# A fused encoder block on one core: turning the next tile's input before the query projection, router steps right behind their turns, and a reordered set of first loads

## The reference

```python
hn   = rmsnorm(h, norm_mix)
b_gate, c_gate, x_in, c_q, c_kv, k_pe = split(hn @ w_in)        # 512,512,512,384,256,64
conv = b_gate * dwconv3_causal(c_gate * x_in)
q    = rmsnorm(c_q) @ w_uq  ;  k_nope, v = rmsnorm(c_kv) @ w_ukv # 4 heads; q, k normed per head, rope
attn = softmax(q k^T / sqrt(192), chunk-causal) v
h    = h + concat([conv, attn]) @ w_o
h    = h + MoE(rmsnorm(h))      # router on 32 experts, the best 4, clamped SwiGLU, gates from a softmax
```

## Time and profile before

| | us |
|---|---|
| median of 3 runs (lowest to highest) | 2258.73 (2258.47 to 2261.2) |
| profiled execution, its own time | 2259.32 |
| its span | 2257.5 |
| PE busy / PEld busy | 2088.5 / 1886.0 |
| DVE / ACT / POOL busy | 738.0 / 443.9 / 556.3 |
| mean granted clock | 0.971 |

### The profile page before, as it was taken

How to read it: one execution, slowest core, us unless ns; L and a number is a source line. 1 busy time by engine, 2 the same in 40 slices (tenths; PEclk the granted TensorE clock), 3 DMA queues, 4 the chain that set the end, 5 groups by cost and what they waited for, 6 DMA issues and landing times.

```text
span 2257.5 us, 41903 instructions
## 1 busy us (share of the span) xinstructions
PE 2088.5 (93%) x15574; PEld 1886.0 (84%) x15575; DVE 738.0 (33%) x1949; ACT 443.9 (20%) x1078; POOL 556.3 (25%) x637
## 2 busy tenths in 40 slices
PE   6888889999994999999999999999999999999991
PEld 5666666675553899999999999999999999999991
DVE  1222222233343333433333333333333433343331
ACT  1222233232321111111111111111111111111110
POOL 1111101110024223232322323223232322323321
PEclk9999999999996999999999999999999999999996
DMA  7000000033421889999999999999999989999997
GB/s 264 10 10 10 10 10 10 1 124 91 130 67 37 279 275 311 325 302 290 291 294 277 305 301 277 317 287 305 287 307 315 320 275 277 316 319 318 306 292 86
DMA packets 308020, 486.97 MB, mean 216 GB/s; under 512 B 107984, under 2 KB 129360, under 8 KB 307920
## 3 DMA queue, kind: packets, MB, share of 16 engines
q1 hardware_dynamic: 250608, 437.49, 59.4%
q0 software_dynamic: 33120, 44.91, 9.6%
q10 hardware_dynamic: 24240, 3.85, 1.1%
HBM read 454.83 MB, written 35.84 MB: 217 GB/s over the span
## 4 chain that ended last, share of the span: by engine, by line
PE 90%; DVE 3%; issue 2%; ACT 2%; DMA 1%; POOL 1%; ACTq 0%; DVEq 0%; SPq 0%; POOLq 0%
PE psum L989 42%; PE psum L1005 22%; PE psum L790 8%; PE psum L938 5%; PE psum L825 2%; PE psum L881 2%; PE psum L828 2%; PE psum L918 2%; PE psum L897 2%; PE psum L805 1%; PE psum L870 1%; PE psum L896 1%; DMA area<-in_w_in 1%; PE psum L968 1%; DVE area L1115 0%
## 5 line engine op out<-in xcount | busy, mean ns | idle before, releaser
L989 PE MATMUL psum<-area 128*128 128x128 f32 (+3 forms) x8192 | 978.8, 282 | 36.5 <-issue 18.8
L989 PEld LDWEIGHTS psum<-area 128*128 128x128 f32 x8192 | 970.3, 192 | 41.8 <-issue 41.5
L1005 PE MATMUL psum<-area 128*128 128x128 f32 (+3 forms) x4096 | 496.3, 282 | 0.9
L1005 PEld LDWEIGHTS psum<-area 128*128 128x128 f32 x4096 | 484.5, 191 | 10.0 <-DVE area L1285 8.7
L1266 DVE TENSOR_SCALAR area<-psum,area 128x160 f32<-128x160 f32 x256 | 86.4, 379 | 612.6 <-PE psum L989 612.6
L588 POOL DMA_INDIRECT sum_rows<-area x165 | 261.1, 1582 | 67.3 <-issue 40.2
L749 ACT ACTIVATE area<-area 128x320 f32<-128x320 f32 x128 | 60.1, 470 | 734.2 <-DVE area L1266 734.2
L790 PE MATMUL psum<-area 128*128 128x128 f32 x1536 | 175.9, 275 | 3.5 <-ACT area L662 1.2
L790 PEld LDWEIGHTS psum<-area 128*128 128x128 f32 x1536 | 173.4, 192 | 5.0 <-ACT area L666 1.7
L578 POOL DMA_INDIRECT area<-normed_rows,area x165 | 160.5, 973 | 61.4 <-issue 61.4
L573 POOL TENSOR_TENSOR area<-area 128x5 uint32<-128x5 uint32 x33 | 6.3, 190 | 620.8 <-DVE area L1251 575.0
(11 more groups left out here) (180 smaller groups left out, 1314.0 us busy)
## 6 DMA issues: line engine op xcount, KB each, us to landing
area<-in_w_gate_up SPq DMA_DIRECT2D x256, 1024.0 KB, 6.5
area<-in_w_down SPq DMA_DIRECT2D x128, 1024.0 KB, 7.1
area<-in_w_in SPq DMA_DIRECT2D x3, 2048.0 KB, 13.0
area<-in_x SPq DMA_DIRECT2D x9, 512.0 KB, 11.1
area<-in_w_o SPq DMA_DIRECT2D x1, 4096.0 KB, 13.1
sum_rows<-area SPq DMA_DIRECT2D x32, 128.0 KB, 3.0
normed_rows<-area SPq DMA_DIRECT2D x8, 512.0 KB, 3.3
out<-sum_rows SPq DMA_DIRECT2D x4, 1024.0 KB, 13.9
```

The costliest lines, as they stand in the source:

```text
L989: ins = mm(dst, w_gu[piece][:, k, c * P:(c + 1) * P], xT[:, PART * s + k, 0:width], start=(s == 0 and k == 0 and c % 2 == 0), stop=(s == 1 ...
L1005: ins = mm(bank[4 + d // 3][:, (d % 3) * SLOTS:(d % 3) * SLOTS + width], w_dn[q][:, kk, d * P:(d + 1) * P], actT[:, 2 * q + kk, 0:width], ...
```

## The change

Four things change. (1) In the loop over the tiles, HNa and HNb of the next tile stand before UQ, HNa between TPa and S, HNb behind PV, and UKV follows UQ directly. The last PV of a tile stands behind X. (2) At the end, the router step RT of a tile stands right behind its turns HB, ahead of the second half of WO. (3) SyncE's first loads: the constants come in two pieces (the first holds the identity and eps), the low block of `w_in` in two halves of four k-rows, each with a semaphore, and the large blocks follow at once. g_mix is issued by ScalarE, the seven small loads by GpSimd, which then waits for `w_ukv` before it writes the zeros and lists. LOW takes the k-rows by halves for both banks. (4) ScalarE does a small Sqrt before anything else. The zeros are taken from `attnT` instead of `v_sb`, so that the wait for their writes moves from UKV(0) on ScalarE to PV(3) on VectorE.

The diff, cut to its core; left out are the declarations of the new semaphores, the other small loads (moved in the same manner), and waits on `rest_in` before the first ranks and before VectorE's use of the token numbers:

```diff
@@ constants
         "ident": np.eye(P, dtype=np.float32),
+        "eps": np.full((P, 1), EPS, np.float32),
...
@@ schedule(), the loop over the eight token tiles
         if i > 1:
-            steps += unit(old + 3)[1:]
+            steps += unit(old + 3)[1:-1]
         steps.append(("X", i))
+        if i > 1:
+            steps.append(("PV", old + 3))
...
         steps.append(("BC", i))
         if i:
-            steps += unit(new)
+            steps.append(("TPa", new))
         if i + 1 < NT:
             steps.append(("HNa", i + 1))
         if i:
-            steps.append(("SC", new + 1))
-        steps.append(("UQ", i))
+            steps += unit(new)[1:]
         if i + 1 < NT:
             steps.append(("HNb", i + 1))
-        steps.append(("UKV", i))
+        if i:
+            steps.append(("SC", new + 1))
+        steps += [("UQ", i), ("UKV", i)]
...
-    steps += [("WO", 4), ("RT", 0), ("HA", 1), ("HB", 1), ("WO", 5), ("RT", 1), ("HA", 2)]
+    steps += [("WO", 4), ("RT", 0), ("HA", 1), ("HB", 1), ("RT", 1), ("WO", 5), ("HA", 2)]
     for i in range(3, e):
-        steps += [("WO", 2 * i), ("HB", i - 1), ("WO", 2 * i + 1), ("RT", i - 1), ("HA", i)]
+        steps += [("WO", 2 * i), ("HB", i - 1), ("RT", i - 1), ("WO", 2 * i + 1), ("HA", i)]
@@ SyncE
             sp.dma_start(xt, x_rows[0]).then_inc(x_in, 16)
-            sp.dma_start(consts[:], consts_dram).then_inc(consts_in, 16)
-            sp.dma_start(g_mix[:], I["norm_mix"][0].rearrange("(k p) -> p k", p=P), allow_slow_non_contiguous=True).then_inc(g_mix_in, 16)
-            sp.dma_start(w_in[:, :, 3 * CONV:], w_in_v[:, :, 3 * CONV:]).then_inc(w_low_in, 16)
-            sp.dma_start(g_q[:, 0:NCQ], I["q_norm"][0].rearrange("(k p) -> p k", p=P), allow_slow_non_contiguous=True).then_inc(small_in, 16)
...
+            sp.dma_start(consts[:, 0:P + 1], consts_dram[:, 0:P + 1]).then_inc(consts_in, 16)
+            for k in (0, KD // 2):
+                sp.dma_start(w_in[:, k:k + KD // 2, 3 * CONV:], w_in_v[:, k:k + KD // 2, 3 * CONV:]).then_inc(w_low_in[2 * k // KD], 16)
+            sp.dma_start(consts[:, P + 1:], consts_dram[:, P + 1:]).then_inc(rest_in, 16)
             sp.dma_start(w_in[:, :, CONV:2 * CONV], w_in_v[:, :, CONV:2 * CONV]).then_inc(w_c_in, 16)
@@ GpSimd
+            g.memset(stat[:, 39:40], 0.0).then_inc(warm_ready, 1)
...
-            zeros = v_sb[:, 0:2, :].rearrange("p a n -> p (a n)")
+            zeros = attnT[:, HEADS - 1, :]
             g.memset(zeros, 0.0).then_inc(zero_ready, 1)
             wait(zero_ready, 2)
+            pool.dma_start(g_q[:, 0:NCQ], I["q_norm"][0].rearrange("(k p) -> p k", p=P), allow_slow_non_contiguous=True).then_inc(small_in, 16)
...
+            wait(w_ukv_in, 16)
             for dram in (hf_dram, acc_dram):
...
-            wait(consts_in, 16)
+            wait(rest_in, 16)
             wait(small_in, 16 * 7)
@@ ScalarE
+            act.dma_start(g_mix[:], I["norm_mix"][0].rearrange("(k p) -> p k", p=P), allow_slow_non_contiguous=True).then_inc(g_mix_in, 16)
+            act.wait_ge(warm_ready, 1)
+            A(stat[:, 38:39], stat[:, 39:40], ACT.Sqrt)
             act.wait_ge(consts_in, 16)
...
-                    if n == 0:
-                        act.wait_ge(zero_out, 16 * 4)
@@ VectorE, step PV
+                    if n == HEADS - 1:
+                        dve.wait_ge(zero_out, 16 * 4)
@@ TensorE, step LOW
-                    for k in range(KD):
-                        mm(bank[2][:, 0:QL], hnT[:, k, :], w_in[:, k, 3 * CONV:3 * CONV + QL],
-                           start=(k == 0), stop=(k == KD - 1))
...
+                    for half in range(2):
+                        if n == 0:
+                            pe.wait_ge(w_low_in[half], 16)
+                        for bk, a, b in ((bank[2], 0, QL), (bank[3], QL, LOW)):
+                            for k in range(4 * half, 4 * half + 4):
+                                ins = mm(bk[:, 0:b - a], hnT[:, k, :], w_in[:, k, 3 * CONV + a:3 * CONV + b],
+                                         start=(k == 0), stop=(k == KD - 1))
```

More of the change, by code:

```diff
@@ L346, in build @@
         w_dn_v = I["w_down"][0].rearrange("e (k p) n -> e p k n", p=P)
-        consts_in, g_mix_in, small_in, x_in = sem("consts_in"), sem("g_mix_in"), sem("small_in"), sem("x_in")
-        w_low_in, w_c_in, w_x_in, w_b_in, w_uq_in, w_ukv_in = (sem(n) for n in ("w_low_in", "w_c_in", "w_x_in", "w_b_in", "w_uq_in", "w_ukv_in"))
+        consts_in, rest_in, warm_ready = sem("consts_in"), sem("rest_in"), sem("warm_ready")
+        g_mix_in, small_in, x_in = sem("g_mix_in"), sem("small_in"), sem("x_in")
+        w_low_in = [sem(f"w_low_in{half}") for half in range(2)]
+        w_c_in, w_x_in, w_b_in, w_uq_in, w_ukv_in = (sem(n) for n in ("w_c_in", "w_x_in", "w_b_in", "w_uq_in", "w_ukv_in"))
         x_sq, in_std, in_rstd, hn_ready = sem("x_sq"), sem("in_std"), sem("in_rstd"), sem("hn_ready")
@@ L519, in rotate @@
                 return g.tensor_tensor(dst, tmp[:, 0:heads * ROPE], tmp[:, heads * ROPE:2 * heads * ROPE], ALU.add)
-            zeros = v_sb[:, 0:2, :].rearrange("p a n -> p (a n)")
+            zeros = attnT[:, HEADS - 1, :]
             g.memset(zeros, 0.0).then_inc(zero_ready, 1)
             wait(zero_ready, 2)
+            pool.dma_start(g_q[:, 0:NCQ], I["q_norm"][0].rearrange("(k p) -> p k", p=P), allow_slow_non_contiguous=True).then_inc(small_in, 16)
+            pool.dma_start(g_q[:, NCQ:], I["kv_norm"][0].rearrange("(k p) -> p k", p=P), allow_slow_non_contiguous=True).then_inc(small_in, 16)
+            pool.dma_start(gq_row[:], I["q_head_norm"].to_broadcast([P, QKH])).then_inc(small_in, 16)
+            pool.dma_start(gk_row[:], I["k_head_norm"].to_broadcast([P, QKH])).then_inc(small_in, 16)
+            for j in range(TAPS):
+                pool.dma_start(taps[:, j, :], I["conv_w"][0, j].rearrange("(k p) -> p k", p=P), allow_slow_non_contiguous=True).then_inc(small_in, 16)
+            wait(w_ukv_in, 16)
             for dram in (hf_dram, acc_dram):
@@ L819, in _ @@
                     pe.wait_ge(hnT_ready, 2 * n + 2)
-                    if n == 0:
-                        pe.wait_ge(w_low_in, 16)
-                    else:
+                    if n:
                         pe.wait_ge(q_normed, n * HEADS)
-                    for k in range(KD):
-                        mm(bank[2][:, 0:QL], hnT[:, k, :], w_in[:, k, 3 * CONV:3 * CONV + QL],
-                           start=(k == 0), stop=(k == KD - 1))
-                    for k in range(KD):
-                        ins = mm(bank[3][:, 0:KVL + ROPE], hnT[:, k, :], w_in[:, k, 3 * CONV + QL:],
-                                 start=(k == 0), stop=(k == KD - 1))
+                    for half in range(2):
+                        if n == 0:
+                            pe.wait_ge(w_low_in[half], 16)
[3 more added lines that the diff above has]
+                                         start=(k == 0), stop=(k == KD - 1))
                     ins.then_inc(low_done, 1)
```

8 lines of the change are left out of this document (2 added, 6 removed).

## The result

The changed kernel takes 2222.53 us (median of 4 runs, 2221.91 to 2227.06), the kernel before 2259.64 in the same rounds: a ratio of 0.9834, 95% interval 0.9822 to 0.9845. It is faster by 37.1 us instead of 47.6, and lies 1.5 us above the predicted range. The span went from 2257.5 to 2220.7, the mean granted clock from 0.971 to 0.974. TensorE's first expert matmul moved from 726.48 to 689.22; behind it the two profiles take 1531.0 and 1531.5.

| stretch | gained, predicted | gained, measured |
|---|---|---|
| start to the end of BC(0) | 1.8 | -1.7 |
| tile 0, BC(0) to LOW(1) | 4.4 | 4.2 |
| tiles 1 to 7, LOW(1) to UQ(7) | 37.9 | 39.6 |
| UQ(7) to WO(0) | 0 | -4.4 |
| WO(0) to the experts | 3.5 | -0.5 |

The account below looks back on a forecast made before the run. PE, busy 93% of the span and holding 90% of the chain, was taken as the bound. 46.8 - 1.4 - 3.1 - 1.7 + 3.1 + 2.1 + 1.8 = 47.6 us off 2259.3 gave 2211.7, median 2211, range 2202 to 2221.

Parts of the forecast that it names:

- UKV behind UQ: Tiles 0 to 6: copying before UQ removes 33.4 us of idling and 13.4 of low clock, gain 46.8 us.
- HNb's waits: HNb's turn waits for VectorE's copy of HNa, 1.1 us in tile 0 and 0.3 in tile 1: cost 1.4.
- PV behind X: X in six tiles waits for ScalarE's last copy of QR's turns: cost 3.1 us, bounds 0 to 4.5.
- rival 2: Behind UKV, ScalarE's lateness reaches the next PV, 0.5 to 1 us in seven tiles: 2216 us; chance 0.15.
- rival 3: The clock stays low somewhere in every tile, so 13.4 us are not gained: 2224.6 us; chance 0.08.
- rival 4: GpSimd's small loads land late and hold up VectorE's part of LOW(0), then CT(0): slower than before; chance 0.03.
- The start: Up to BC(0): LOW(0) starts earlier, but GpSimd's wait for w_ukv holds BC(0); net gain 1.8 us, bounds -1.1 to 3.7.
- rival 1: At the start GpSimd's wait does not decide: gain 9.5 us instead of 1.8, 2203.5 us; chance 0.1.
- Short waits leave the granted clock at 2.4 GHz: TensorE's clock stays high behind short waits, read from two matmuls taking 0.49 us behind a wait of 1.94.
- RT(6): Last router step, ahead of WO's second half: gain 3.1 us in waits and 2.1 from the clock (0 to 4.2).
- RT(1): Front of the router steps: the first ranks wait at once for tile 0's mask, 1.7 us lost.
- The rule of the Trainium skill: Many small idle gaps between matmul groups make the clock swing; by it UKV's 13.4 us would not come back.

Follow-up runs that it names:

- best_tail: Changed kernel with late GpSimd writes, PV before X, old router order, idle matmuls in two waits, and 164 semaphore increments ahead of experts: 2213.98 us, ratio 0.9789.

## Why the prediction was wrong

- **UKV behind UQ (46.8), HNb's waits (1.4), PV behind X (3.1): right.** The order of the tiles brings what the sum said, and 1.7 more between LOW(1) and UQ(7). HNb waits 0.9 in tile 0 and not at all in tile 1. PV behind X costs 2.3 by the run that undoes it; the waits for L677 are 4.0 in all, where the waits of X were 1.1 before. Rivals 2, 3 and 4 are out: PV's waits for ScalarE behind UKV are what they were (1.38 instead of 1.39 ahead of LOW(2), then 0.96 and 0.53), no UKV has a low clock, and the seven small loads land 5.7 to 7.5 us after their issue, all by 16 us.
- **The start (+1.8): failed in size and sign, the mechanism was right.** This is a mis-sized term, 3.5 us; at -1.7 it lies below its own lower bound of -1.1. `w_ukv` landed at 40.8 (24.29 + 16.5) instead of 38.3, near the upper bound of 41.2; from there to BC(0) it took 6.4 instead of 6.0; and the low clock in BC(0) cost 2.3 instead of 1.7. The landing is 6.4 us behind what 386 GB/s give. I had put 3.9 there, where the kernel before has 6.8, with nothing to show that its slow stretches would go. They did not: from 2 to 12 us the DMA engines moved 267 GB/s on the mean (207 from 4 to 6 and 218 from 8 to 10 us), and 333 in the kernel before. The short rows of the small loads were in flight then, which may be the cause and was not tested apart. That GpSimd's wait decides is shown by the run with late writes, and rival 1 is out. Even without that wait BC(0) begins at 41.14, 6.6 us earlier than before and not rival 1's 9.5.
- **"Short waits leave the granted clock at 2.4 GHz": the step that failed.** It was read off one wait of 1.94 us, and the sum priced the clock behind every wait of TensorE that stayed, or was new, at nothing, but for 2.1 us coming back at RT(6). The full clock there was luck: behind this very wait the clock fell in four of eleven profiles. And the two matmuls that I read it from take 0.49 either way. The trace of before had a counterexample too, the wait of 3.19, with 16 matmuls in 3.56 us behind it instead of 2.01. Measured: 4.4 lost behind a wait of 2.35 in tile 7 that was there before, with its matmuls at the full clock then; 1.9 lost behind the new wait of RT(1); 1.6 won behind a wait of 3.19. Together -4.7 where the sum had 0. The waits of 2.35 and 3.19 did not change: what differs is whether the granted clock falls behind them, and the same instructions show both. So the -4.4 and the +1.6 are what these two profiles happened to show, and another pair may give other sizes. The 1.9 at RT(1) was no chance, the clock fell there each time. Whatever the two came to, the forecast had no term for them.
- **RT(6) (3.1 for the waits and 2.1 for the clock): too large.** From the turns to WO it became 2.2 shorter, and WO 0.5 longer, so 1.7 instead of 5.2. I had named VectorE's copy of HB(6) as the last to come. The longest of the waits left is the router's first half for ScalarE's copy of HA (L724, at 633.36), which stands behind a square root and its table load:

```profile
631.87 1.28 ACT L740 ACT_TABLE_LOAD   x1
633.16 0.29 ACT L740 ACTIVATE attn_stat<-attn_stat 128x1 f32<-128x1 f32 x1
633.36 0.58 ACT L724 ACTIVATE area<-psum 128x512 f32<-128x512 f32 x1
```

- **The rule of the Trainium skill** that I weighed against this (TensorE: Matmul & The Clock Gate, "A second HAM failure mode: psum-queue depth-cycling") tells of a kernel in which frequent small idle gaps between groups of matmuls make the clock swing. In tiles 1 to 6, where I priced it at 13.4 us, the trace of the changed kernel does not bear it out: 28.8 us for L891. What the runs do show, falls behind single waits of 1.69 to 3.19 us, is another case than many small gaps.
- **RT(1) (1.7): right** at 1.69 for the wait; the clock behind it is counted above.

The steps add up: of the 10.4 us missing between 47.6 and 37.2, the start has 3.5, the clock behind waits 4.7, RT(6) 3.5 and smaller ones 0.4, less the 1.7 that the tiles gave beyond the sum.

What stays open: why the clock falls behind one wait of 2.35 us and not behind the same one 0.36 us later, and whether the loads as a whole cost 4 us or 1.

## What to carry over

A reorder that lets a copy be done before its buffer is asked for is worth its idle time plus the low clock behind it, and both can be read from the groups by line. Price a wait like those of 1.7 to 3.2 us here as one behind which the granted clock may or may not fall, in a range and not by one row; and when a wait is put into an engine's stream, look at everything queued behind it. Whoever adds instructions ahead of a long loop should look at the instruction queue's line of the page before judging the edit: 92 instructions can cost 100 us that have nothing to do with them.

## What the runs showed of the hardware

Instructions come in transfers of 16.4 KB (0.59 MB in 36, 1.39 MB in 85), and 256 more instructions took one more. A shift of 92 instructions made the loop over the experts fetch again and again, with waits of up to 23.0 us; a shift of 256 did not. The Trainium skill (Advanced Engine Details and Errata, "ISA Cache") gives lines of 16 KB, 256 instructions each, and for TensorE 128 KB of them. The transfers agree with the size of a line; the 128 KB no run here shows. The reading that the shifted loop touches one line more than is held fits, but how many lines the loop spans was not measured.

An increment of a semaphore on TensorE took some 0.15 us: TensorE's first matmul starts at 14.99 behind 92 of them and at 25.97 behind 164, with no other wait at the head, and the 164 ahead of the experts stand for 26.57. So padding is not free. The forecast for `best_tail` took only the 15.6 us of delay for the increments' price, and had them fit into a wait of 17.67.
